# Packed small inputs, feature-major x and keys, and an unrolled last turn of the expert loop, in a two-layer hybrid MoE step on one core

## What is computed

```python
h = rmsnorm(x, norm_mix) * (1 + scale1) + shift1          # modulation from silu(cond) @ w_ada + b_ada
mix = retention(h) | diff_attention(h) | mla(h)           # all from h @ w_in; caches and states for the sample
x = x + gate1 * (mix @ w_out)
h = rmsnorm(x, norm_ffn) * (1 + scale2) + shift2
x = x + gate2 * (routed(h) + shared(h))                   # 64 experts, 6 per token, sigmoid router
```

## Time and profile before

| | |
|---|---|
| median of 3 executions | 1529.07 us (1528.58 to 1530.09) |
| the profiled execution, its own time | 1525.73 us |
| its span, first to last instruction | 1523.9 us |
| TensorE busy | 1333.0 us (87%), 9920 matmuls and as many weight loads |
| VectorE, ScalarE busy | 301.4 us, 240.5 us |
| loaded | 493.08 MB, on average 325 GB/s over the span |
| mean granted TensorE clock | 0.916 of full speed |

### The profile page before, as it was taken

The page is one execution under the profiler, slowest core; times in us unless marked ns, Lnnn a source line. Parts: engine busy times, 40 slices in busy tenths (PEclk is TensorE's granted clock), DMA queues, the critical chain, the costliest instruction groups (busy, mean ns, idle before and its releaser), DMA issues.

```text
span 1523.9 us, 23671 instructions
## 1 busy us (share of the span) xinstructions
PE 1333.0 (87%) x9920; PEld 918.7 (60%) x9920; DVE 301.4 (20%) x718; ACT 240.5 (16%) x503; POOL 3.1 (0%) x18
## 2 busy tenths in 40 slices
PE   5799988998898888899879978899898888898885
PEld 3555678865565455566556557886665455566554
DVE  1115413311110110111041452331110110111012
ACT  1102622010110000010020252201110001010101
POOL 0000000000000000000000000000000000000000
PEclk9799878999999989999989997999999899999998
DMA  9766734578999999999963571446899999999991
GB/s 341 261 228 267 280 143 193 203 309 359 423 422 423 422 422 415 420 423 423 423 230 112 234 305 56 175 196 277 355 421 423 422 409 421 422 423 422 423 421 66
DMA packets 89229, 495.74 MB, mean 325 GB/s; under 512 B 17760, under 2 KB 21088, under 8 KB 33120
## 3 DMA queue, kind: packets, MB, share of 16 engines
q1 hardware_dynamic: 84976, 492.58, 79.3%
q10 hardware_dynamic: 4208, 2.52, 0.5%
HBM read 493.08 MB, written 2.00 MB: 325 GB/s over the span
## 4 chain that ended last, share of the span: by engine, by line
PE 58%; DMA 26%; SPq 6%; DVE 4%; issue 3%; ACT 3%; DVEq 0%; ACTq 0%
DMA gu<-in_exp_w_up 25%; PE PS L1852 15%; PE PS L1480 10%; PE PS L1808 6%; PE PS L1815 6%; PE PS L1874 6%; PE PS L1729 4%; PE PS L1406 3%; SPq L506 2%; SPq L520 2%; ACT xh L844 2%; SPq L450 2%; PE PS L1712 1%; PE PS L1790 1%; PE PS L1457 1%
## 5 line engine op out<-in xcount | busy, mean ns | idle before, releaser
L1852 PE MATMUL PS<-gu,arena 128*32 128x256 f32 (+1 forms) x3456 | 355.0, 432 | 108.1 <-DMA gu<-in_exp_w_up 106.4
L1852 PEld LDWEIGHTS PS<-gu,arena 128*32 128x32 f32 (+1 forms) x3456 | 193.9, 131 | 218.3 <-DMA gu<-in_exp_w_up 116.0
L1808 PE MATMUL PS<-arena 128*128 128x128 f32 x1472 | 184.1, 278 | 0.5 <-ACT arena L895 0.5
L1808 PEld LDWEIGHTS PS<-arena 128*128 128x128 f32 x1472 | 171.8, 192 | 18.5 <-issue 17.5
L1815 PE MATMUL PS<-arena 128*128 128x256 f32 x704 | 164.5, 388 | 12.1 <-issue 12.1
L1874 PE MATMUL PS<-dn,arena 128*32 128x512 f32 (+1 forms) x864 | 160.4, 596 | 0.0
L1815 PEld LDWEIGHTS PS<-arena 128*128 128x128 f32 x704 | 133.8, 195 | 31.5 <-issue 14.2
L1852 PE MATMUL PS<-xh,arena 128*64 128x256 f32 x640 | 143.0, 381 | 0.0
L1336 DVE TENSOR_TENSOR arena<-arena,PS 128x256 f32<-128x256 f32 x44 | 18.5, 421 | 599.3 <-ACT arena L892 599.3
L1852 PEld LDWEIGHTS PS<-xh,arena 128*64 128x64 f32 x640 | 85.5, 137 | 61.3 <-issue 16.8
L880 ACT ACTIVATE arena<-PS 128x512 f32<-128x512 f32 x88 | 52.5, 597 | 350.1 <-PE PS L1874 350.1
(11 more groups left out here) (236 smaller groups left out, 918.4 us busy)
## 6 DMA issues: line engine op xcount, KB each, us to landing
gu<-in_exp_w_gate SPq DMA_DIRECT2D x108, 1024.0 KB, 8.9
gu<-in_exp_w_up SPq DMA_DIRECT2D x108, 1024.0 KB, 14.7
dn<-in_exp_w_down SPq DMA_DIRECT2D x108, 1024.0 KB, 20.2
gu<-in_w_ada SPq DMA_DIRECT2D x24, 2048.0 KB, 10.0
xh<-in_exp_w_gate SPq DMA_DIRECT2D x20, 1024.0 KB, 21.3
xh<-in_exp_w_up SPq DMA_DIRECT2D x20, 1024.0 KB, 22.5
arena<-in_exp_w_down SPq DMA_DIRECT2D x20, 1024.0 KB, 16.1
gu<-in_w_in SPq DMA_DIRECT2D x8, 2048.0 KB, 16.2
```

The source lines that it names most:

```text
L1808: ins = mmul(PS[:, 4, (c % 4) * P:(c % 4) * P + P], h_tok[:, g, c], onehot[b][:, g], start=(g == 0), stop=(g == 1))
L1852: ins = mmul(PS[w * h:w * h + w, 5, FF * half:FF * half + FF], xg[:, k, w * h:w * h + w], weights[:, half, k], start=(k == 0), stop=(k == ...
```

## The change

Three things are changed.

1. **Inputs.** The host lays 20 small inputs out in three arrays: `packed_x` (x, already feature-major, straight to `xT`, 1 MB), `packed_first` (constants, conditioning, biases and gains, 968 KB) and `packed_late` (caches with the keys feature-major, states, rows, 1.6 MB). The transposes of x and of the caches, their copies out, and the waits for them go. Columns of `w_out` and `sh_w_down` are reordered on the host, so that the weights of a chunk lie side by side.
2. **Last turn.** The loop runs over `TURNS - 1` turns. The last quad and pair rounds are written out behind it. The overflow pass stands between them, with buffers of its own. The last pair round has no gather, and the final scatter follows it directly.
3. **First quad.** Its loads are issued by halves: gate, up and down of slots 0 and 1, then those of slots 2 and 3.

```diff
-            sp.dma_start(x_tok[:, 0], t["x_prompt"][0]).then_inc(S["const_in"], 16)
-            sp.dma_start(x_tok[:, 1], t["x_sample"][0]).then_inc(S["const_in"], 16)
-            sp.dma_start(cst[:, :], t["shape_consts"]).then_inc(S["const_in"], 16)
...
+            sp.dma_start(xT[:, :, :].rearrange("p c t -> p (c t)"), t["packed_x"]).then_inc(S["x_in"], 16)
+            sp.dma_start(cst[:, :], t["packed_first"]).then_inc(S["const_in"], 16)
...
                     if n == RING + 1:
-                        small_loads()
+                        sp.dma_start(late[:, :], t["packed_late"]).then_inc(S["small_in"], 16)
...
-                for part in range(3):
-                    for j in range(4):
-                        if j % 2 == 0:
-                            sp.wait_ge(used[part], r0 + j // 2 + 1)
-                        load_quad(j, l, xs[j], part)
+                for h in range(2):
+                    for part in range(3):
+                        sp.wait_ge(used[part], r0 + h + 1)
+                        for j in (2 * h, 2 * h + 1):
+                            load_quad(j, l, xs[j], part)
...
-                if l == 0:
-                    turn_caches()
...
-                wo = [piece(("w_out", l, i)).rearrange("p (k t c) -> p k c t", k=4, c=NC_) for i in range(2)]
+                wo = [piece(("w_out", l, i)).rearrange("p (k c t) -> p k c t", k=4, c=NC_) for i in range(2)]
...
-                wd = dn[:, RING - 1].rearrange("p j (t c) -> p j c t", c=NC_)
+                wd = dn[:, RING - 1].rearrange("p j (c t) -> p j c t", c=NC_)
...
-                    pe.wait_ge(S["sel_ready"], m * 2 + ((ROUNDS + 2) * l + u + 2))
-                    gather(1 - b, 0).then_inc(S["gathered"], 1)
+                    if not last:
+                        pe.wait_ge(S["sel_ready"], m * 2 + (r0 + u + 2))
+                        gather(1 - b, 0).then_inc(S["gathered"], 1)
...
-                    turn_pair().then_inc(S["turned"], 1)
-                    pe.wait_ge(S["xg_a"], m * 2 + (g0 + u + 2))
-                    gather(1 - b, 1).then_inc(S["gathered"], 1)
+                    turn_pair(gated).then_inc(S["turned"], 1)
+                    if not last:
+                        pe.wait_ge(S["xg_a"], m * 2 + (g0 + u + 2))
+                        gather(1 - b, 1).then_inc(S["gathered"], 1)
...
-                with pe.Fori(0, TURNS) as m:
...
-                pe.wait_ge(S["y_out"], 2 * (r0 + ROUNDS))
+                with pe.Fori(0, TURNS - 1) as m:
+                    quad(m)
+                    pair(m)
+                quad(TURNS - 1)
                 o = ov[l]
-                pe.wait_ge(S["xg_b"], (ROUNDS + 1) * (l + 1))
                 with pe.If(over_flag(pe, l) > 0):
...
+                pair(TURNS - 1, last=True)
+                pe.wait_ge(S["y_out"], 2 * (r0 + ROUNDS))
                 scatter(told=S["combined"])
```

More of the change, by code:

```diff
@@ L59 @@
 PER_TURN = 6
-COLUMNS = E + PER_TURN
 def quad_at(m):
@@ L915, in _ @@
                                 results(n).then_inc(o["y"], 1)
+                hidden_and_results(TURNS - 1, 3, last=True)
             for b in range(4):
@@ L1937, with laid_out, by_partition @@
          ("ret_bwd", (1, DEPTH, RET_H, RET_D, RET_D))]
+PACKED = ("x_prompt", "x_sample", "c_ctx", "c", "b_ada", "norm_mix", "norm_ffn", "cache_diff_k", "cache_diff_v",
+          "cache_mla_ckv", "cache_mla_kpe", "state_ret_fwd", "state_ret_bwd", "router_bias", "diff_subln", "mla_kv_norm",
+          "mla_q_norm", "diff_lambda", "ret_decay_fwd", "ret_decay_bwd")
+def laid_out(i):
+    def by_partition(a):
+        a = a.reshape(-1, P, NC_)
+        return a.transpose(1, 0, 2).reshape(P, -1)
+    x = np.concatenate([i["x_prompt"][0], i["x_sample"][0]], axis=0)
+    x = x.reshape(T, P, NC_).transpose(1, 2, 0).reshape(P, NC_ * T)
+    first = [shape_constants(), by_partition(i["c_ctx"]), by_partition(i["c"]), by_partition(i["b_ada"]),
+             by_partition(i["norm_mix"]), by_partition(i["norm_ffn"])]
+    kpe = np.zeros((P, DEPTH, P), np.float32)
+    kpe[MLA_N:MLA_QK] = i["cache_mla_kpe"][0].transpose(2, 0, 1)
+    k = i["cache_diff_k"][0].reshape(DEPTH, 2, 2, P, 2 * DIF_D).transpose(2, 4, 0, 1, 3)
+    states = np.stack([i[n][0].reshape(DEPTH, 2, 2, RET_D, RET_D) for n in ("state_ret_fwd", "state_ret_bwd")])
+    rows = np.concatenate([i[n].reshape(DEPTH, -1) for n in ("router_bias", "diff_subln", "mla_kv_norm", "mla_q_norm",
+                                                             "diff_lambda", "ret_decay_fwd", "ret_decay_bwd")], axis=1)
+    late = [k.reshape(P, -1), i["cache_diff_v"][0].transpose(2, 0, 1, 3).reshape(P, -1),
+            i["cache_mla_ckv"][0].transpose(2, 0, 1).reshape(P, -1), kpe.reshape(P, -1),
+            states.transpose(3, 4, 1, 2, 0, 5).reshape(P, -1),
+            np.broadcast_to(rows.reshape(1, -1), (P, rows.size))]
+    named = {n: a for n, a in i.items() if n not in PACKED}
+    for n in ("w_out", "sh_w_down"):
+        a = i[n]
+        named[n] = a.reshape(*a.shape[:-1], P, NC_).swapaxes(-1, -2).reshape(a.shape)
+    named["packed_x"], named["packed_first"] = x, np.concatenate(first, axis=1)
+    named["packed_late"] = np.concatenate(late, axis=1)
+    return named
 def kernel(**inputs):
@@ L1945 @@
     arrays, t, out = {}, {}, {}
-    for name, value in [*inputs.items(), ("shape_consts", shape_constants())]:
+    for name, value in laid_out(inputs).items():
         a = np.ascontiguousarray(value)
```

216 lines of the change are left out of this document (77 added, 139 removed).

## The result

The changed kernel took 1488.55 us (median of 4 executions, 1486.55 to 1492.03) against 1529.48 for the kernel before beside it. The ratio is 0.9735, with a 95% interval of 0.9717 to 0.9753, so 41 us or 2.65% faster. The forecast was 1492.7. The profiled execution took 1486.98 with a span of 1485.2, so 38.7 us of span less than before (1523.9).

The account below looks back on a forecast made before the run. It took the weight stream to bound the turns and TensorE's own work nearly all the rest. 15.9 + 7.2 + 1.1 + 12.2 = 36.4 us gave 1489.3 profiled, 1492.7 for the median; 8 in 10 for 1482 to 1506.

Parts of the forecast that it names:

- the likeliest case, one stall: The forecast itself, 1493 us: the moved jump over the overflow block stalls in one layer, layer 1; chance 0.5.
- The start: Program start to the end of the second w_in piece: earlier weight stream and fuller clock gain 15.9 us.
- The first step: Up to the first w_in piece: the fourth w_ada piece arrives at 27.5, not 31.72, gaining 4.2 us.
- the second: First w_in piece's start to the second's end: 32.9 us instead of 44.5, 11.6 less, of which 2.7 is clock.
- w_out and shared down: Weight loads without the stride hide behind matmuls: 5.7 us in w_out, 1.5 in shared down, both layers, 7.2 together.
- First quad: First expert turn: loads by halves bring the ups earlier, gaining 0.6 us in layer 0 and as much in layer 1; 1.1.
- Last turn: Last rounds without gather and with the jump moved: 10.9 us in layer 0, 1.3 in layer 1, together 12.2.
- The place of the targets: Overflow jump's targets: some 130 instructions into a code piece in layer 0, right behind a seam in layer 1.
- The 1.5 us taken for layer 0: Stall assumed at the moved jump in layer 0, between the last quad's downs and the last pair's gates.
- the pause of 7 us: Behind layer 0's last results, before the final scatter: taken as the jump over the overflow block, gone when it moves.
- The rule weighed in the forecast: Taken strictly, it charges the overflow jump in both layers, as in the first rival: 30.4 us gained, 1499; chance 0.2.

Follow-up runs that it names:

- experiment 3: The changed kernel with only 400 of the first pack's 1,936 columns loaded first, the rest ahead of the late pack; 1485.70 us, ratio 0.9712 to the kernel before.
- experiment 10: The changed kernel with the first pack loaded in 10 column slices and the late pack in 26, same bytes; 1490.40 us, ratio 0.9755 to the kernel before.
- experiment 2: The changed kernel with the late pack of small inputs loaded as 26 column slices instead of one load; 1491.18 us, ratio 0.9753 to the kernel before.
- experiment 1: The changed kernel with the old column order of w_out and sh_w_down; 1498.53 us, ratio 0.9791 to the kernel before.
- experiment 4: The changed kernel with the first quad's loads in the old order (all gates, ups, downs), not by halves; 1488.85 us, ratio 0.9727 to the kernel before.
- experiment 7: The changed kernel with the old last turn: loop runs all turns, last round gathers, overflow pass and jump behind it; 1487.47 us, ratio 0.9742 to the kernel before.
- experiment 11: The kernel before with 98 empty increments placed where TensorE waits, only moving its code; 1515.41 us, ratio 0.9920 to the kernel before.
- experiment 5: The changed kernel with 150 never-executed instructions added to layer 0's overflow pass on TensorE; 1488.42 us, ratio 0.9734 to the kernel before.
- experiment 8: The changed kernel with empty instructions at TensorE's start, in layer 0's pass and layer 1's last quad, moving both jump targets; 1485.07 us, ratio 0.9731.
- experiment 6: The changed kernel with 100 empty increments between gates and ups of layer 1's last quad; 1489.01 us, ratio 0.9752 to the kernel before.

## Why the forecast was right, and where it was not

**In all.** 36.4 us forecast, 38.7 in the profiled span, 40.9 between the medians; the likeliest case, one stall, is the one that came. The parts below add up to 38.4: 18.3 + 6.7 + 13.7 + 1.7, less 2.0 net in the turns and their first quad. Misses of both signs meet in the sum, so part of its closeness is luck.

**The start: 15.9 forecast, 18.3 measured.** The first step was sized 4.2 and gave 5.2; the second 11.6, and gave 13.1. In the first the fourth `w_ada` piece came at 28.23, 0.7 later than forecast, but from there to the first `w_in` piece it took 5.9 us and not the 7.65 that were to stay: the piece's own matmuls ran at full clock (1.97 us; 3.56 before, at 0.53 of full speed). In the second the first `w_in` piece ran 15.6 us instead of the 17.0 assumed. That is luck of the clock: it took 16.7 to 17.0 in eight of the twelve profiled kernels behind the change, and 15.6 to 15.7 in four. The mechanism stands: experiments 3 and 10 show the start bound by the bytes and issues ahead of `w_ada`. Why the pause behind the first `w_in` piece went is shown only in part (experiments 2 and 10).

**w_out and shared down: 7.2 forecast, 6.7 measured** (2.9 and 1.8 in `w_out`, 1 a layer in the other). Experiment 1 shows the stride as the cause. `w_out` in layer 1 fell short (30.82 us, where seven of the ten experiments with the new columns took 29.2 to 29.5), by the same wandering clock.

**First quad: 1.1 forecast; nothing was kept.** Pair 0 of layer 0 starts 51.87 us behind the first expert round (324.97 - 273.10), and started 52.65 behind it in the chain of the kernel before:

```profile
348.64 7.08 PE PS L1852 x64
```

So 0.8 us a layer are there when pair 0 starts. But up to the end of the last quad the turns, bound by the weight stream, are 2.2 and 1.3 us longer than before and take it back with more. The forecast said itself that a gain inside the turns pays nothing, and still added this one. That is the term that failed, and experiment 4 shows that the new order wasn't even what took the wait away in layer 0.

**Last turn: 12.2 forecast, 13.7 measured.** Layer 0 gave 11.0 (10.9 forecast) with 0.72 us of stall for 1.5. Layer 1 gave 2.7 (1.3) with 4.10 us and 1.7 of slow clock for 5.0 and 2.5. The place of the targets, worked out from rows, was right within its error: 106 into the next piece (130 said), and right behind a seam one piece further on. The number was right; what it was credited to was incomplete. The forecast had the pause of 7 us and the slow scatter go because the jump left its old place. Experiments 7 and 11 show that in layer 0 they go in the old place too, and split the gain: moving the old code took 6.6 us off A and 4.8 off B with no other change. Gathers and copies left out, and the jump put elsewhere, are worth 3.2 to 4.3 us in A, and 3.6 in B (37.1 in experiment 11 against 33.5 in experiment 5, neither with a long stall). So in layer 0 some two thirds of the gain is that the jump no longer lands 18 instructions ahead of a seam. In layer 1 a stall was exchanged for another. The 1.5 us taken for layer 0 were a guess; 0.72 came because the fetch had begun 2.1 us ahead of the jump.

**Not forecast**: 1.7 us between layer 1's first `w_in` matmul and its `w_out` (150.5 us for 152.2). The same stretch took 150.5 to 155.2 in the experiments, so I don't ascribe it.

**The rule weighed in the forecast.** The Trainium skill (Runtime: NRT & Kernel Launch, "Instruction fetch mechanics") gives pieces of 256 instructions, and a stall for a taken branch outside a window of two pages. Forward the trace agrees in kind: a target two pieces on costs 4.1 to 4.4 us (4.06, 4.10, 4.39), and one in the next piece 0 to 1.9 us at the jump, by how early that piece's fetch began. So the forecast read the rule too strictly for layer 0, whose target it put in the next piece. Backward the trace doesn't agree: the loop's jump goes back three pieces with no fetch. Taken strictly the rule would have charged each of the loop's jumps back, and there was no fetch in 347 us of them.

**The range.** The lower bounds of the four terms add up to 17 us and the upper ones to 49, where the forecast says 20 and 48. No chance hangs on it.

## What to carry to other kernels

Look at the "issue" pieces of the chain beside the instruction fetches, and count where the target of each taken forward jump lies in the compiled code. Here it cost at most 1.3 us where the target was in the next piece, well ahead of its end, and that piece's fetch began some 2 us or more ahead of the jump. That was so for jumps 35 or more instructions into their own piece, and for one whose piece the loop had already entered. Otherwise it cost 1.9 to 5.5 us, and mostly the clock behind it. Do this count before crediting a gain to an edit that also moves code; undoing the edit alone would have misled here, and moving the code alone told it. A gain that ends ahead of a stretch bound by the weight stream is not to be added to the sum.

## What the runs showed of the hardware

**A jump's landing place can cost more than the jump.** Landing 18 and 17 instructions ahead of a seam, TensorE stopped for 5.45 us (kernel before, layer 0) and for 2.19 behind the first 1.12 (experiment 7, layer 1): the first records of the target ran, and then the next piece was missing. After a jump the next piece's fetch begins up to 3.7 us later (the jump at 729.64, the fetch at 733.32 in the changed kernel), and what it brings runs 2.4 us or more after that. 66 instructions up to the seam were enough in experiment 7, where the scatter waits for VectorE in between; 18 and 17 were not; and 86, in experiment 8's block of matmuls without waits, fell 0.25 us short.

**From a fetch to its first record.** The pauses of the table above ended 2.37 to 2.80 us after the start of the fetch, whatever their own length (0.25 to 5.45 us).

**The clock wanders between executions of the same code.** From 144 to 205 us the changed kernel and experiment 8 run the same attention code; windows (length, busy of five engines, granted clock, DMA share, GB/s) of the one and of the other:

```profile
144.00:205.00 61.00, 56.75 (x378) 45.43 (x379) 21.99 (x42) 24.86 (x65) 0.00 (x0) 0.81 0.55 215
```
```profile
144.00:205.00 61.00, 55.70 (x337) 43.98 (x338) 20.97 (x38) 25.35 (x69) 0.00 (x0) 0.64 0.56 223
```

0.81 against 0.64 of full speed, with part of the stretch at 1.2 GHz in both. From the first `w_in` matmul to `w_out` in layer 0 the twelve profiled kernels behind the change took between 159.3 and 168.0 us, and in layer 1 from the start of `w_out` to the first expert round between 75.4 and 81.2 (experiment 1, with its slower columns, aside). This is why single edits of 1 to 5 us were read from intervals around their place and not from the totals, and why experiments 5 to 8 leave the total nearly where it was.
